# One expert stage of a hybrid decoder layer: gathers and transposes cut from whole 128-row tiles to each expert's own row count

## The reference, cut to what matters

```python
logits = xf @ router_w + router_b                 # xf: 1024 normalised tokens
top_val, top_idx = lax.top_k(logits, 4)
gates = softmax(top_val)
# for each expert e, over the tokens x that chose it:
gu = x @ w_gu[e] + b_gu[e]                        # 1024 -> 2048
gate, up = split(gu, 2)
gate = minimum(gate, 7); up = clip(up, -7, 7)
y = ((up + 1) * (gate * sigmoid(1.702 * gate))) @ w_down[e] + b_down[e]
out[token] += y * gate_weight
```

## Time and profile before

| | |
|---|---|
| median of 3 runs | 2281.06 us (2280.94 to 2282.16) |
| profiled execution | 2280.05 us |
| its span | 2278.3 us |
| PE busy | 2214.6 us, 97% |
| PE weight loads | 1832.8 us, 80% |
| VectorE, ScalarE, GpSimd busy | 747.3, 372.1, 586.4 us |
| moved by DMA | 505.81 MB, 222 GB/s over the span |

### The profile page before, as it was taken

How to read it: one execution, slowest core, us unless ns; L and a number is a source line. 1 busy time by engine, 2 the same in 40 slices (tenths; PEclk the granted TensorE clock), 3 DMA queues, 4 the chain that set the end, 5 groups by cost and what they waited for, 6 DMA issues and landing times.

```text
span 2278.3 us, 45334 instructions
## 1 busy us (share of the span) xinstructions
PE 2214.6 (97%) x18872; PEld 1832.8 (80%) x18873; DVE 747.3 (33%) x1759; ACT 372.1 (16%) x845; POOL 586.4 (26%) x808
## 2 busy tenths in 40 slices
PE   8999998999996999999999999999999999999997
PEld 5665446678765989898898989889898898898975
DVE  2234777454632172222222222222222222213223
ACT  2222653223220101010100101001010010110102
POOL 1133222322423122222222223222232223222312
PEclk9999999999997999999999999999999999999999
DMA  8000113011017788888989799998999979899897
GB/s 266 1 0 19 21 36 154 19 47 47 29 38 252 265 266 279 289 268 275 297 273 319 237 337 296 293 322 284 306 302 293 334 243 336 272 349 351 261 322 285
DMA packets 381977, 505.81 MB, mean 222 GB/s; under 512 B 19248, under 2 KB 295284, under 8 KB 381720
## 3 DMA queue, kind: packets, MB, share of 16 engines
q1 hardware_dynamic: 362632, 459.58, 60.3%
q0 software_dynamic: 19136, 43.29, 7.1%
HBM read 472.19 MB, written 33.05 MB: 222 GB/s over the span
## 4 chain that ended last, share of the span: by engine, by line
PE 73%; SPq 5%; issue 2%; DVE 2%; DMA 1%; POOL 1%; ACT 0%; DVEq 0%; ACTq 0%; POOLq 0%
PE ps L1787 37%; PE ps L1815 12%; PE ps L1800 8%; PE ps L1213 5%; PE ps L1036 3%; SPq L784 3%; PE ps L1765 2%; SPq L1545 1%; PE ps L1774 1%; PE ps L1128 1%; DMA arena<-h_dram,arena 1%; PE ps L1069 1%; SPq L1555 1%; DMA arena<-h_dram 1%; PE ps L1044 0%
## 5 line engine op out<-in xcount | busy, mean ns | idle before, releaser
L1787 PEld LDWEIGHTS ps<-arena 128*64 128x64 f32 (+1 forms) x12544 | 961.6, 152 | 20.0 <-issue 17.7
L1787 PE MATMUL ps<-arena 128*64 128x108 f32 (+29 forms) x12544 | 973.9, 273 | 2.5 <-issue 1.7
L1957 DVE TENSOR_SCALAR arena<-ps,arena 128x108 f32<-128x108 f32 (+29 forms) x256 | 92.3, 361 | 1062.4 <-PE ps L1787 1058.4
L1622 POOL TENSOR_TENSOR arena<-arena 128x108 f32<-128x108 f32 (+29 forms) x256 | 133.1, 520 | 1076.0 <-DVEq L1964 1076.0
L1815 PE MATMUL ps<-arena 128*128 128x224 f32 (+14 forms) x1920 | 273.4, 303 | 0.2 <-POOL arena L1625 0.2
L1697 ACT ACTIVATE arena<-arena 128x108 f32<-128x108 f32 (+29 forms) x256 | 81.5, 318 | 1172.5 <-DVE arena L1957 1172.5
L1815 PEld LDWEIGHTS ps<-arena 128*128 128x128 f32 x1920 | 270.4, 189 | 1.0 <-POOL arena L1625 0.4
L1800 PE MATMUL ps<-arena 128*128 128x512 f32 x544 | 238.6, 596 | 2.7 <-POOL arena L1625 2.7
L1800 PEld LDWEIGHTS ps<-arena 128*128 128x128 f32 x544 | 102.5, 191 | 126.7 <-issue 121.6
L536 PE MATMUL ps<-arena 128*128 128x384 f32 (+1 forms) x512 | 171.5, 494 | 2.1 <-DVE arena L639 2.1
L536 PEld LDWEIGHTS ps<-arena 128*128 128x128 f32 x512 | 97.4, 193 | 68.2 <-issue 2.6
(11 more groups left out here) (275 smaller groups left out, 1591.0 us busy)
## 6 DMA issues: line engine op xcount, KB each, us to landing
arena<-in_exp_w_gu SPq DMA_DIRECT2D x256, 1024.0 KB, 10.4
arena<-in_exp_w_down SPq DMA_DIRECT2D x64, 2048.0 KB, 11.6
arena<-in_exp_b_down SPq DMA_DIRECT2D x17, 512.0 KB, 10.1
arena<-in_x SPq DMA_DIRECT2D x16, 512.0 KB, 8.9
arena<-in_w_in SPq DMA_DIRECT2D x8, 1024.0 KB, 9.6
h_dram<-arena SPq DMA_DIRECT2D x16, 512.0 KB, 2.8
arena<-in_w_out SPq DMA_DIRECT2D x1, 4096.0 KB, 14.2
arena<-h_dram SPq DMA_DIRECT2D x8, 512.0 KB, 13.5
```

Source lines behind the costliest of these rows:

```text
L1622: v.tensor_tensor(gmn[m % 2][:, 0:n], gmn[m % 2][:, 0:n], umn[m % 2][:, 0:n], ALU.mult).then_inc(S("gum", m % 2), 1)
L1787: last = t_.matmul(bank(m % 4)[c0:c1, q * CAP:q * CAP + n], wslot[g][:, k, 256 * q + c + c0:256 * q + c + c1], xT[:, k, 0:n], start=(k == ...
L1957: v.tensor_scalar(gmn[r][:, 0:n], bank(m % 4)[:, 0:n], of[:, m:m + 1], LIMIT, ALU.add, ALU.min).then_inc(S("gmn", r), 1)
```

## The change

The gathers, the transposes in, VectorE's copies behind them and the transposes out take the number of rows n of the expert in place of the number of tiles. Each tile handles p = min(128, n - 128 j) rows. The first tile of a wide expert stays at 128 rows. The lists are not altered, nor are the products, the scatters and the weight loads, nor the order of any engine's work. In all, the gathers fetch 4394 rows in place of 6016.

```diff
             for j in range(TILES[0]):
-                pool.indirect_dma_start(xin[:, j, :], None, h2_dram,
-                                        bass.IndirectOffsetOnAxis(ap=idx[0][:, j, 0:1], axis=0)).then_inc(S("xin", j), 16)
+                p = min(P, ROWS[0] - j * P)
+                pool.indirect_dma_start(xin[0:p, j, :], None, h2_dram,
+                                        bass.IndirectOffsetOnAxis(ap=idx[0][0:p, j, 0:1], axis=0)).then_inc(S("xin", j), 16)
...
-            def gather(to, tiles):
+            def gather(to, n):
                 pool.sem_inc(S("gathering"), 1)
-                for j in range(tiles):
-                    pool.indirect_dma_start(xin[:, j, :], None, h2_dram,
-                                            bass.IndirectOffsetOnAxis(ap=to[:, j, 0:1], axis=0)).then_inc(S("xin", j), 16)
+                for j in range(-(-n // P)):
+                    p = min(P, n - j * P)
+                    pool.indirect_dma_start(xin[0:p, j, :], None, h2_dram,
+                                            bass.IndirectOffsetOnAxis(ap=to[0:p, j, 0:1], axis=0)).then_inc(S("xin", j), 16)
...
-            def rows_in(b, before, wide, tiles):
-
-                for j in range(tiles):
+            def rows_in(b, before, wide, n):
+
+                for j in range(-(-n // P)):
+                    p = min(P, n - j * P)
                     pe.wait_ge(S("xin", j), 16 * (wide if j else b) + 16)
                     for r in range(2):
                         if j == 1:
                             pe.wait_ge(S("gu_bank", r), 2 * b + 1)
                         for k in range(4):
-                            last = t_.transpose(bank(4 * (1 - j) + r)[:, k * P:(k + 1) * P],
-                                                xin[:, j, (4 * r + k) * P:(4 * r + k + 1) * P], ident)
+                            last = t_.transpose(bank(4 * (1 - j) + r)[:, k * P:k * P + p],
+                                                xin[0:p, j, (4 * r + k) * P:(4 * r + k + 1) * P], ident[0:p, 0:p])
                         last.then_inc(S("xT_ps", r), 1)
 
-            def rows_out(j, b, before):
-
+            def rows_out(j, b, before, n):
+
+                p = min(P, n - j * P)
                 for r in range(2):
                     pe.wait_ge(S("tr_bank", r), before + (j + 1))
                     for k in range(4):
-                        last = t_.transpose(bank(6 + r)[:, k * P:(k + 1) * P], yv[:, 4 * r + k, j * P:(j + 1) * P], ident)
+                        last = t_.transpose(bank(6 + r)[0:p, k * P:(k + 1) * P], yv[:, 4 * r + k, j * P:j * P + p], ident)
                     last.then_inc(S("yt_ps", r), 1)
...
-                        v.tensor_tensor(xT[:, 4 * r:4 * r + 4, j * P:(j + 1) * P], heads(bank(4 * (1 - j) + r)),
-                                        over_cols(ffng_T[:, 4 * r:4 * r + 4]), ALU.mult).then_inc(S("xT_sb"), 1)
+                        v.tensor_tensor(xT[:, 4 * r:4 * r + 4, j * P:j * P + p], heads(bank(4 * (1 - j) + r))[:, :, 0:p],
+                                        over_cols(ffng_T[:, 4 * r:4 * r + 4], p), ALU.mult).then_inc(S("xT_sb"), 1)
```

More of the change, by code:

```diff
@@ L1595, in load_main @@
                 load_list(idx[r], main_expert(pool, r) * STRIDE, r % 4)
-            def gather(to, tiles):
+            def gather(to, n):
                 pool.sem_inc(S("gathering"), 1)
-                for j in range(tiles):
-                    pool.indirect_dma_start(xin[:, j, :], None, h2_dram,
-                                            bass.IndirectOffsetOnAxis(ap=to[:, j, 0:1], axis=0)).then_inc(S("xin", j), 16)
+                for j in range(-(-n // P)):
+                    p = min(P, n - j * P)
+                    pool.indirect_dma_start(xin[0:p, j, :], None, h2_dram,
+                                            bass.IndirectOffsetOnAxis(ap=to[0:p, j, 0:1], axis=0)).then_inc(S("xin", j), 16)
             def gather_main(r):
                 pool.wait_ge(S("idx_in", r % 4), 16 * (r // 4 + (r % 4 > 0)))
-                gather(idx[r], TILES[r])
+                gather(idx[r], ROWS[r])
             def scatter(rows, b, n, of=yt):
@@ L1683, in _ @@
                 pool.wait_ge(S("idx_in", 0), 16 * i + 16 * (NE // 4))
-                gather(idx[0], 2)
+                gather(idx[0], CAP)
                 gated(i + NE, CAP, lambda m: None)
@@ L1823, in rows_out_main @@
                     pe.wait_ge(S("yv"), 8 * wide_to(r) + 8)
-                    rows_out(0, r, tiles_to(r))
+                    rows_out(0, r, tiles_to(r), ROWS[r])
                 if m == 4:
-                    rows_out(1, r, tiles_to(r))
-            rows_in(0, 0, 0, TILES[0])
+                    rows_out(1, r, tiles_to(r), ROWS[r])
+            rows_in(0, 0, 0, ROWS[0])
             for r in range(NE):
@@ L1832, in _ @@
                 if r + 1 < NE:
-                    rows_in(r + 1, tiles_to(r + 1), wide_to(r + 1), TILES[r + 1])
+                    rows_in(r + 1, tiles_to(r + 1), wide_to(r + 1), ROWS[r + 1])
                 if TILES[r] == 2:
@@ L1840, in _ @@
             with each_more(pe, lambda: None, lambda: pe.sem_inc(S("exp_end"), 1)) as i:
-                rows_in(i + NE, 2 * i + TALL, i + WIDE, 2)
+                rows_in(i + NE, 2 * i + TALL, i + WIDE, CAP)
                 pe.wait_ge(S("xT_sb"), 4 * i + (2 * TALL + 4))
@@ L1846, in _ @@
                 for j in range(2):
-                    rows_out(j, i + NE, 2 * i + TALL)
+                    rows_out(j, i + NE, 2 * i + TALL, CAP)
         @block.vector
@@ L1926, in plan_more, with rows_in @@
                 dve.sem_inc(S("more_ready"), 1)
-            def rows_in(before, tiles):
-                for j in range(tiles):
+            def rows_in(before, n):
+                for j in range(-(-n // P)):
+                    p = min(P, n - j * P)
                     for r in range(2):
                         dve.wait_ge(S("xT_ps", r), before + (j + 1))
-                        v.tensor_tensor(xT[:, 4 * r:4 * r + 4, j * P:(j + 1) * P], heads(bank(4 * (1 - j) + r)),
-                                        over_cols(ffng_T[:, 4 * r:4 * r + 4]), ALU.mult).then_inc(S("xT_sb"), 1)
+                        v.tensor_tensor(xT[:, 4 * r:4 * r + 4, j * P:j * P + p], heads(bank(4 * (1 - j) + r))[:, :, 0:p],
+                                        over_cols(ffng_T[:, 4 * r:4 * r + 4], p), ALU.mult).then_inc(S("xT_sb"), 1)
                 dve.sem_inc(S("xin_free"), 1)
@@ L2011, in tiles_between @@
                         tile_scale(t, 0)
-            rows_in(0, TILES[0])
+            rows_in(0, ROWS[0])
             for r in range(NE):
@@ L2019, in _ @@
                 if r + 1 < NE:
-                    rows_in(tiles_to(r + 1), TILES[r + 1])
+                    rows_in(tiles_to(r + 1), ROWS[r + 1])
                 if r == 1:
@@ L2064, in _ @@
             with each_more(dve, last_rows, all_again) as i:
-                rows_in(2 * i + TALL, 2)
+                rows_in(2 * i + TALL, CAP)
                 biases(more_expert(dve, i), eb[0])
```

## The result

| | median of the runs, us | ratio to before, 95% interval | profiled execution, us |
|---|---|---|---|
| before | 2281.36 (2280.46 to 2284.35, 6 runs) | 1 | 2280.05, span 2278.3 |
| after | 2290.47 (2288.92 to 2294.67, 6 runs) | 1.0042 [1.0032, 1.0052] | 2290.02, span 2288.3 |

The change makes the kernel slower, by 9.1 us in the medians. I had forecast 7.5 us faster, and the time lies outside my range.

A forecast was written before the change was run, and what follows sets the result against it. TensorE, busy 97% of the span, was taken as the bound; savings of 1.3 + 5.4 + 0.8 = 7.5 us gave 2272.5 us profiled, 2273.5 median. Range 2270.5 to 2284, the forecast's own 2271 to 2276.5.

The forecast's parts named there:

- The next wait would be for weights: Expert stage: if TensorE's work shrinks, it would next wait for weights, with the DMA share going from 0.89 to 1.06.
- A microsecond taken from PE in this stage is a microsecond off the end: Expert stage: TensorE's savings shorten the whole kernel one for one, as long as the next wait is not late.
- The price of a transpose: Wide experts' second tiles: 60 ns taken as what loading 128 columns costs each narrowed transpose, bounds 41 and 112.
- the 1.4 that I named: Chain ahead of a narrow expert's down product: 16 transposes should take about 1.4 us in place of 1.90.
- my 5.4 + 1.3: Transposes in: 5.4 us saved on wide experts' second tiles, 1.3 us on narrow experts' tiles.
- as I said of widths 156 to 132: Wide experts' down products wait for the last hT slice from GpSimd, so 0.43 us of transpose saving is lost.
- my 0.8: First expert, width 224, second tile uncovered on the path: transposes 0.4 to 0.5 us and gather 0.3, together 0.8.
- Rows out, evictions: Transposes out (L1774): no saving, group stays at 32.8 us; VectorE's shorter evictions worth nothing beyond the first expert.
- rival 1: Gathers on few DMA queues make weights late: stalls of some 4 to 9 us, 2277.5 to 2282.5, chance 0.21.
- rival 2: Gathers on few DMA queues at the upper price: 15 to 25 us of weight stalls, 2288 to 2298, chance 0.12.
- The margins of TensorE's weights, 7.1 and 9.1 us: Late expert stage: how early weights land before use, 7.1 us behind the scatter of 118, 9.1 for the last expert.
- 32 came back in 265 us: Late expert stage: weight margin recovered between the two readings despite scatters of 122 and 124 rows, 12 us in 100.

The follow-up runs named there:

- the run with the transposes alone: The kernel after with whole gathers of 128 rows, only transposes and their evictions cut: 2278.48 us, 0.9983 of before.
- rounding to 16: The kernel after with each gather's row count rounded up to the next multiple of 16: 2280.24 us, 0.9990 of before.
- The gathers alone: The kernel after with transposes and evictions whole again, only the gathers narrowed: 2293.94 us, 1.0046 of before.
- the run with three widths: The kernel after with three late WIDTHS raised, 124 and 122 to 126 and one 118 to 120: 2274.18 us, 0.9970 of before.

## Why the prediction was wrong, point by point

**What bounds the kernel.** The first failed step is the sentence "The next wait would be for weights". I read the shares and the chain inside the stage and didn't follow the chain to the end, where before already shows it on SyncE's queue from 2126 us to the load of h at 2234.06. The resource without a margin was this queue, and its last customers were not weights but the loads of h, 8 x 512 KB, with ScalarE, GpSimd and the last down product behind them. "A microsecond taken from PE in this stage is a microsecond off the end" was thus not true of the last expert: there PE waited for hT (2.7 us before) and ScalarE 7.1 us for h.

**Transposes in.** The price of a transpose was nearly right: by the records a small one follows the last after some 62 to 66 ns (I took 60), whatever its rows. By shape, 8 transposes of tiles of 76, 40 and 4 rows, with the last one's drain in it, and of 118 for comparison (two tiles there):

```profile
L1768 PE MATMUL ps<-cst,arena 76*128 76x76 f32 x8 | 0.7, 229 | 0.0
...
L1768 PE MATMUL ps<-cst,arena 40*128 40x40 f32 x8 | 0.7, 232 | 0.0
...
L1768 PE MATMUL ps<-cst,arena 4*128 4x4 f32 x8 | 0.7, 202 | 0.0
...
L1768 PE MATMUL ps<-cst,arena 118*128 118x118 f32 x16 | 1.9, 264 | 0.0
```

The term was mis-sized around it. For second tiles of 56 rows and fewer, the first narrowed transpose starts 203 ns after the last whole one, the next 84 to 111 ns after that, and the down product 127 to 160 ns after the last narrowed one, so that 16 take 1.62 to 1.66 us and not the 1.4 that I named. And the down product gives back 0.10 us behind each of them. The second tiles of 76 and 68 rows have no such gap (109 ns to the first, as between whole ones): they save 0.35 and 0.37 us where the smaller ones save 0.14 to 0.19, and 0.04 and 0.05 come back. What sets the two apart wasn't tried. Over experts 1 to 26, the run with the transposes alone against before, from start to start: the 13 second tiles save 2.55 us and 1.21 come back in the down products, the 13 first tiles save 1.66 and 1.09 come back. That leaves 1.3 + 0.6 us, less 0.2 lost in gate products of narrow experts, for my 5.4 + 1.3. From expert 0's to expert 25's gate products the four profiles with whole transposes take 1239.4 to 1240.9 us and six with narrowed ones 1237.6 to 1239.6: 1.5 us between the means. That a wide expert's down product waits its saving away, as I said of widths 156 to 132, holds from width 168 down, and for most of it at 184 and 176. Why a narrow expert's takes 0.10 us longer, with its eighth hT slice long there, wasn't tried. The first expert gives 0.56 us for my 0.8: its transposes take 1.56 us for 1.99 and the copy behind them 0.57 for 0.70, but the gather of 96 rows isn't faster than that of 128 (8.26 us for 7.63), so the 0.3 that I had put there is nothing.

On the rule of the Trainium skill that I weighed (TensorE: Matmul & The Clock Gate, section LDWEIGHTS, columns over 1.2 GHz): the measurement decides against it for these transposes, which load 128 columns and follow each other after some 62 ns where it gives 107.

**Rows out, evictions.** Right: 32.8 to 32.2 us, no part of the loss.

**Gathers, and rivals 1 and 2.** The mechanism was right in each of its signs, and priced at nothing in the forecast: the narrowed gathers of 106, 118 and 122 rows start slower (1.7 us for 1.0) and land late, and those of widths that divide well don't. That agrees with the rule of the Trainium skill (DMA: Bandwidth & Descriptors, section on why a DMA increments its semaphore by 16), now for gathers too, and rounding to 16 takes the loss away. Three sizes and a place were wrong. The added delay is 13.5 us for the 122 rows (20.3 for 6.8), between the 10 that I took and the 20 of rival 2. The margins of TensorE's weights, 7.1 and 9.1 us, were nearly enough: one stall of 3.2 us, at the lower edge of rival 1's. "32 came back in 265 us" holds for weights early; after 2126 nothing comes back to SyncE's queue, which neither rival has. And the chances, 0.33 for the two together against 0.52 for the saving, set a term of 7.5 us that rested on an assumed pitch above a mechanism for which the scatters gave direct rows.

**The reckoning.** The gathers alone give +0.46% [0.34, 0.58], 10.5 us. The transposes alone give -0.17% [-0.26, -0.09], 3.9 us, of which the two profiles show 1.4: 0.56 ahead of expert 0's gate products and 0.8 from there to the end of the span (1562.9 us for 1563.7). Expert 31's gate products start 1.8 us earlier (1503.9 us after expert 0's, for 1505.7), but the loads of h only 0.6, and TensorE's waits for the last down product grow from 2.7 to 4.1: even what TensorE did save was in part waited away at SyncE's queue. The sum is +0.29%, where the change measured +0.42% [0.32, 0.52]; the intervals cover the difference.

## What to carry to other kernels

Before an operand of an indirect DMA is cut to its exact size, look at what the count divides by: one gather of 122 rows in place of 128 cost 5.5 us, while in the run with three widths a gather of 126 rows for the same expert landed after 8.2 us. Follow the chain of the last 100 us to its end before pricing anything: a queue that issues back to back there turned a delay, however far from TensorE, into time, and such a delay 280 us earlier was free. A small saving on the busiest engine is worth looking for in the next instruction's duration too, since here over half of it came back there.

## What was not expected of the hardware

A transpose of 4 to 76 rows by 128 columns costs the same, 0.7 us for 8, and from 56 rows down the change of shape costs about 0.1 us before and up to 0.05 behind: 203 ns to the first one, 127 to 160 ns to the product behind, where whole ones have 109. A gather of 118 or 122 rows, half a megabyte, lands 18 to 25 us after its issue where 128 rows take 7, or 17 to 24 right behind a slow scatter. And the issue of a load by SyncE, 0.4 and 1.2 us for a pair of quarters early in the stage, takes 2.7 us and more in most cases late in the stage of both kernels (13.5 for a load of down weights at 2126 us before), and at most 1.4 where no late transfer has a count that divides badly, so that the issuing engine itself became the chain.
